# Two FFNs with 512-column up matmuls, a convolution that reads SBUF, one-tensor decay levels and other banks for the first output projection

## What is computed

```python
def first_block(x, ...):
    ...
    og = gla_attention(gq, gk, gv, split_heads(log_a, GLA_HEADS))      # gated linear attention
    ...
    x = x + jnp.concatenate([y_moba, y_gla], axis=-1) @ w_out[l]       # output projection, "out1"
    hn = rms_norm(x, ffn_norm_g[l])
    h = causal_dwconv(hn @ w_ffn_up[l], conv_w[l], conv_b[l])          # 1024 -> 2 * 2816, then 3 taps over tokens
    h_gate, h_val = h[..., :D_FF], h[..., D_FF:]
    x = x + (jax.nn.silu(h_gate) * h_val) @ w_ffn_down[l]              # "ffn1"
    return rms_norm(x, final_norm_g)

def _swiglu(x, w_in, w_out):                                           # second block, "ffn2"
    g, u = jnp.split(x @ w_in, 2, axis=-1)
    return (jax.nn.silu(g) * u) @ w_out
```

## Time and profile before

| | |
|---|---|
| time, median of 3 runs (lowest to highest) | 782.22 us (782.15 to 782.26) |
| the profiled execution: its time, its span | 782.25 us, 780.4 us |
| TensorE clock granted, mean over the span | 0.988 of full speed |
| busy: TensorE matmul, weight load, VectorE, ScalarE, GpSimd | 753.9, 707.7, 468.2, 371.2, 56.6 us |
| chain that ended last: TensorE, VectorE, ScalarE | 91%, 5%, 2% |

### The profile page before, as it was taken

How to read it: one execution, slowest core, us unless ns; L and a number is a source line. 1 busy time by engine, 2 the same in 40 slices (tenths; PEclk the granted TensorE clock), 3 DMA queues, 4 the chain that set the end, 5 groups by cost and what they waited for, 6 DMA issues and landing times.

```text
span 780.4 us, 13423 instructions
## 1 busy us (share of the span) xinstructions
PE 753.9 (97%) x5562; PEld 707.7 (91%) x5562; DVE 468.2 (60%) x533; ACT 371.2 (48%) x441; POOL 56.6 (7%) x63
## 2 busy tenths in 40 slices
PE   8999894999999999999999999999999999999997
PEld 8898883799999999989989999999989999999996
DVE  5669744457667677677447645565675544454542
ACT  6535354346454554555555563544435343434331
POOL 2465400010000000003000000000010000000000
PEclk9999996999999999999999999999999999999999
DMA  8733331335445455542442444445443554545431
GB/s 331 300 108 128 143 110 54 115 113 205 163 167 209 166 210 182 197 162 89 182 162 108 165 160 168 173 167 195 170 179 134 174 206 162 202 174 198 180 108 54
DMA packets 18046, 128.30 MB, mean 164 GB/s; under 512 B 2000, under 2 KB 2256, under 8 KB 2768
## 3 DMA queue, kind: packets, MB, share of 16 engines
q1 hardware_dynamic: 18000, 127.63, 45.3%
HBM read 126.57 MB, written 1.05 MB: 164 GB/s over the span
## 4 chain that ended last, share of the span: by engine, by line
PE 91%; DVE 5%; ACT 2%; issue 1%; POOL 1%; DMA 1%; SPq 0%; DVEq 0%; ACTq 0%
PE ps L1373 29%; PE ps L1374 28%; PE ps L1375 28%; PE ps L1362 1%; DVE low L900 1%; PE ps L1480 1%; DVE h L930 1%; PE ps L1517 1%; DMA cst<-in_cst 1%; PE ps L1510 0%; DVE xlo L947 0%; PE ps L1489 0%; ACT xhi L561 0%; PE ps L1656 0%; POOL st L476 0%
## 5 line engine op out<-in xcount | busy, mean ns | idle before, releaser
L900 DVE TENSOR_TENSOR low<-raw,hiw 128x2048 fp32r<-128x2048 f32 x116 | 271.1, 2338 | 200.1 <-ACT hiw L531 199.7
L1373 PE MATMUL ps<-xhi,hiw 128*128 128x256 f32 x1216 | 346.4, 285 | 3.5 <-DVE xlo L947 1.8
L1374 PE MATMUL ps<-xlo,hiw 128*128 128x256 f32 x1216 | 344.0, 283 | 0.0
L1375 PE MATMUL ps<-xhi,low 128*128 128x256 f32 x1216 | 344.0, 283 | 0.0
L531 ACT ACTIVATE hiw<-raw 128x2048 fp32r<-128x2048 f32 x116 | 221.4, 1911 | 89.8 <-PE ps L1375 89.8
L1373 PEld LDWEIGHTS ps<-xhi,hiw 128*128 128x128 f32 x1216 | 232.9, 192 | 6.5 <-DVE arena L1323 1.9
L1374 PEld LDWEIGHTS ps<-xlo,hiw 128*128 128x128 f32 x1216 | 233.0, 192 | 0.7
L1375 PEld LDWEIGHTS ps<-xhi,low 128*128 128x128 f32 x1216 | 233.0, 192 | 0.0
L1373 PE MATMUL ps<-hiw,yhi 128*128 128x512 f32 x208 | 82.7, 398 | 10.4 <-ACT arena L621 10.4
L1374 PE MATMUL ps<-low,yhi 128*128 128x512 f32 x208 | 82.2, 395 | 0.0
L1375 PE MATMUL ps<-hiw,ylo 128*128 128x512 f32 x208 | 81.9, 394 | 0.0
(11 more groups left out here) (193 smaller groups left out, 723.3 us busy)
## 6 DMA issues: line engine op xcount, KB each, us to landing
raw<-in_slabs SPq DMA_DIRECT2D x117, 1024.0 KB, 4.7
vec<-in_vec SPq DMA_DIRECT2D x1, 1258.5 KB, 9.6
cst<-in_cst SPq DMA_DIRECT2D x1, 1220.0 KB, 13.7
h<-in_x SPq DMA_DIRECT2D x2, 512.0 KB, 3.9
out<-h SPq DMA_DIRECT2D x2, 512.0 KB, 2.6
vec<-in_vec SPq DMA_DIRECT2D x1, 229.0 KB, 5.1
cst<-in_cst SPq DMA_DIRECT2D x1, 66.0 KB, 4.1
```

The costliest lines, as they stand in the source:

```text
L900: dve.tensor_tensor(low[:, n % SPLIT, :], raw[:, n % RAW, :], hiw[:, n % SPLIT, :].bitcast(F32), ALU.subtract).then_inc(lo_made, 1)
L1373: pe.matmul(o, whi, mhi, start=start, stop=False)
L1374: pe.matmul(o, whi, mlo, start=False, stop=False)
L1375: return pe.matmul(o, wlo, mhi, start=False, stop=stop)
```

## The change

- Output projection: the accumulators take banks 0, 1, 3, 4, and the four tiles of the norm behind it banks 2, 5, 6, 7.
- Levels: keys and queries are scaled in place in one tensor, the early half of each block by the keys and the late half by the queries, 256 columns each; `Kl` is gone and TensorE reads both operands from `Dl`.
- Both FFNs: `xhi` and `xlo` become two slices of one tensor `xx`, side by side. An up slab makes for each column half and contraction tile one matmul of 512 columns (high weights by both) and one of 256 columns (low weights by `xhi`, added to the first half of the bank). A hidden tile so takes two banks: 4 and 5 for gate, 6 and 7 for value, in every step. VectorE adds the two halves by a `tensor_reduce` of 1024 columns to 512 in SBUF and gives the banks back.
- First FFN: all three taps then read SBUF (`hid`). Second FFN: silu and product read SBUF (`up`).

```diff
+OUT1_BANKS = (0, 1, 3, 4)
...
-        xhi = sb("xhi", [P, KT, T], F32R)
-        xlo = sb("xlo", [P, KT, T], F32R)
+        xx = sb("xx", [P, KT, 2, T], F32R)
+        xhi, xlo = xx[:, :, 0, :], xx[:, :, 1, :]
...
-            tenant(f"w1_{q}", q, 0)
+            tenant(f"w1_{q}", OUT1_BANKS[q], 0)
         for q in range(4):
-            tenant(f"n1_{q}", 4 + q, 2)
+            tenant(f"n1_{q}", (2, 5, 6, 7)[q], 2)
...
-        FREE = {"ffn1": 2, "ffn2": 1}
+        FREE = {"ffn1": 1, "ffn2": 1}
...
-                    tenants[4 + 2 * (f % 2) + j].append(FREE[k])
+                    tenants[4 + 2 * j].append(FREE[k])
...
-        def hidden(k, f, j):
-            return ps[:, 4 + 2 * (f % 2) + j, :]
+        def wide_hidden(j):
+            return ps[:, 4 + 2 * j:6 + 2 * j, :]
...
                 pool.wait_ge(s("decay"), i + 1)
-                pool.tensor_tensor(Kl[i % 2], Dl[i % 2], gkT, ALU.mult)
-                pool.tensor_tensor(Dl[i % 2], Dl[i % 2], gqT, ALU.mult).then_inc(s("level_scaled"), 1)
+                early, late = level_halves(Dl[i % 2], i)
+                pool.tensor_tensor(early, early, level_halves(gkT, i)[0], ALU.mult)
+                pool.tensor_tensor(late, late, level_halves(gqT, i)[1], ALU.mult).then_inc(s("level_scaled"), 1)
...
-                    act.wait_ge(*hidden_full(k, f, j, i))
                     if k == "ffn1":
+                        act.wait_ge(*hidden_free(k, f, j, i))
...
-                            act.activation(yb[par][:, 2 * j + c, :], hidden(k, f, j)[:, c * T:(c + 1) * T],
+                            act.activation(yb[par][:, 2 * j + c, :], hid[par][j][:, c, :],
                                            ACT.Identity, scale=sc, bias=bi).then_inc(s("tap2"), 1)
                     elif j == 0:
-                        act.activation(sil[par], hidden(k, f, 0), ACT.Silu).then_inc(hidden_free(k, f, 0)[0], 1)
+                        act.wait_ge(*hidden_free(k, f, 0, i))
+                        act.activation(sil[par], up[par][0].rearrange("p a b -> p (a b)"), ACT.Silu)\
+                           .then_inc(s("silu_made2"), 1)
...
                     if k == "ffn1":
 
+                        dve.wait_ge(*hidden_full(k, f, j, i))
+                        dve.tensor_reduce(hid[par][j], wide_hidden(j).rearrange("p c (a b) -> p c b a", a=2), AX_X,
+                                          ALU.add).then_inc(hidden_free(k, f, j)[0], 1)
+                        dve.wait_ge(*hidden_free(k, f, j, i))
                         for c in range(2):
...
-                            dst, src = yb[par][:, 2 * j + c, :], hidden(k, f, j)[:, c * T:(c + 1) * T]
+                            dst, src = yb[par][:, 2 * j + c, :], hid[par][j][:, c, :]
...
+                    else:
+                        dve.wait_ge(*hidden_full(k, f, j, i))
+                        if f >= 2 and j == 0:
+                            dve.wait_ge(s("silu_made2"), f - 1 if i is None else f - 1 + 2 * i)
+                        dve.tensor_reduce(up[par][j], wide_hidden(j).rearrange("p c (a b) -> p c b a", a=2), AX_X, ALU.add)\
+                           .then_inc(hidden_free(k, f, j)[0], 1)
...
-                    dve.tensor_tensor(gt[par], hidden(k, f, 1), sil[par], ALU.mult).then_inc(hidden_free(k, f, 1)[0], 1)
+                    dve.wait_ge(s("silu_made2"), f + 1 if i is None else f + 1 + 2 * i)
+                    dve.wait_ge(*hidden_free(k, f, 1, i))
+                    dve.tensor_tensor(gt[par], up[par][1].rearrange("p a b -> p (a b)"), sil[par],
+                                      ALU.mult).then_inc(s("gated2"), 1)
...
+            def feature_major_wide(banks, n, norm=None):
+
+                hi, lo = slab_views(n, KT)
+                for c in range(2):
+                    o = banks[:, c, :]
+                    cc_ = slice(c * P, (c + 1) * P)
+                    for kt in range(KT):
+                        turned(norm if c == 0 else None, kt)
+                        both = xx[:, kt].rearrange("p a b -> p (a b)")
+                        if kt < KT - 1:
+                            pe.matmul(o, hi[:, kt, cc_], both, start=kt == 0, stop=False)
+                            pe.matmul(o[:, 0:T], lo[:, kt, cc_], xhi[:, kt, :], start=False, stop=False)
+                        else:
+                            pe.matmul(o[:, 0:T], lo[:, kt, cc_], xhi[:, kt, :], start=False, stop=False)
+                            mm = pe.matmul(o, hi[:, kt, cc_], both, start=False, stop=True)
+                return mm
...
-                    q_, k_ = Dl[i % 2], Kl[i % 2]
+                    q_ = k_ = Dl[i % 2]
...
-                    if i is not None or f >= 2 or ffn_lease[k][2 * (f % 2) + j][1]:
-                        pe.wait_ge(*hidden_free(k, f, j, i, done=False))
+                    pe.wait_ge(*hidden_free(k, f, j, i, done=False))
...
-                    feature_major(hidden(k, f, j), n + j, norm if (f, j) == (0, 0) else None).then_inc(hidden_full(k, f, j)[0], 1)
+                    first = norm if (f, j) == (0, 0) else None
+                    up_made = feature_major_wide(wide_hidden(j), n + j, first)
+                    up_made.then_inc(hidden_full(k, f, j)[0], 1)
```

More of the change, by code:

```diff
@@ L352, in build @@
         Dl = [piece(512 * j, 2, T) for j in range(2)]
-        Kl = [piece(1024 + 512 * j, 2, T) for j in range(2)]
         zb, za, ze = (piece(3072 + 512 * j, 2, T) for j in range(3))
@@ L373, in build @@
         gt = [piece(7168 + 512 * j, 512) for j in range(2)]
+        hid = [[piece(8192 + 1024 * j + 512 * k, 2, T) for j in range(2)] for k in range(2)]
+        up = [[piece(4096 + 1024 * j + 512 * k, 2, T) for j in range(2)] for k in range(2)]
         sg = piece(0, 2, KT, T)
```

44 lines of the change are left out of this document (24 added, 20 removed).

## The result

The changed kernel takes 798.12 us (median of 4 runs, 797.30 to 801.42), the kernel before 782.18 (4 runs on the same chip, 782.10 to 782.26): ratio 1.0212, 95% interval 1.0182 to 1.0242. It is 2.1% slower. The forecast was 788.3 with a range up to 797.0: the sign came out, the size did not. The profiled execution took 798.81, its span is 797.0, 16.6 us more than before.

The account below looks back on a forecast made before the run. TensorE's own pace bounds the FFNs before; after the change a VectorE-ScalarE chain bounds the first FFN. From 782.25 us, -12.5 - 3.8 - 4.2 + 24.5 + 2.0 = +6.0 gives 788.3 us, range 781 to 797.

Parts of the forecast that it names:

- Banks, -12.5: Output projection: first slab no longer waits for bank 2, the second starts 12.5 us sooner, clock stays at 2.4 GHz; -12.5 us.
- What follows has the same waits as before: Output projection behind the second slab: a further transpose, two slabs and the norm keep their waits, so 12.5 us is saved.
- Levels, -3.8: Last attention levels: shorter GpSimd products let VectorE deliver sooner, -2.3 us of wait, and the clock doesn't fall; -3.8 us.
- The clock's share: Last levels: TensorE's clock, which fell to half behind the wait, was expected not to fall, worth 1.5 us.
- a wait under 0.6 us: Sign named for the levels: TensorE's wait in the last levels, 2.41 us before, falls under 0.6 us.
- 512-column matmuls in the second FFN, -4.2: Second FFN up slabs: 0.205 us less a slab, 4.5 us in 22 slabs, less 0.3 for tight banks; -4.2 us.
- The price of the tight spots (0.3): Second FFN: up(1) after reduce(0) and up(10) value after reduce(9) wait for single banks; 0.3 us for both.
- First FFN, +24.5 and +2.0: First FFN: VectorE-ScalarE chain of 19.0 us a loop step against TensorE's 16.6, +24.5 us; lower clock at last down slab, +2.0.
- two taps 0.93 (0.505 each): First FFN chain: ScalarE's pair of convolution taps takes 0.93 us, 0.505 each with a little overlap.
- the walk: First FFN chain followed step by step, 18.1 us straight and 19.0 in the loop, until down(10) ends at 374.4 instead of 349.9.
- The rivals with a cheap sum: First FFN: reduce under 0.95 us instead of 1.22; at 0.69 the time is 776.6, or 772.5 with register stops hidden; chance 0.14.
- Half of the projection's gain lost: Output projection rival: its second wait, or the clock, keeps half of the 12.5 us, giving 794.5; counted within slower, 0.78.

## Why the prediction was off

**Banks, -12.5: measured -11.4.** In the changed kernel the first slab started at 115.66, 11.5 us sooner than in the earlier trace rows, the second at 123.02, 13.65 sooner (both include the levels' gain and the later start-up). "What follows has the same waits as before" was wrong. With the slabs early, slab 15's low part on VectorE stood ahead of the third pair of heads, and the values behind them waited 1.1 us more. Moving the heads ahead brought 1.14 us.

**Levels, -3.8: measured -3.1.** The clock's share was right (1.5). The wait shrank by 1.32 in place of 2.3: the prediction let GpSimd be done before VectorE's remainder started, and it still overlapped two instructions of VectorE. The sign named on record, a wait under 0.6 us, did not come.

**512-column matmuls in the second FFN, -4.2: measured -2.5.** A mixed tile takes 0.353 us where 0.347 was taken: 16 x 0.006 is 0.1 of the 0.205 us a slab. The spacing behind a wide up matmul is 237 ns, not the 227 of the down slabs. It is 237 also where another wide one follows, so it isn't the mix of widths that costs the 10 ns; what does isn't shown. The price of the tight spots (0.3) can't be told apart from it. The formula of the Trainium skill, page "TensorE: Matmul & The Clock Gate", section "Back-to-back issue gap", weighed in the prediction, gave 0.9 for this FFN; the measured 2.5 lies about half-way between it and the forecast.

**First FFN, +24.5 and +2.0: measured +31.6.** The mechanism was right in its main steps: a sum of 1.22 us (1217 and 1220 ns measured), a chain across VectorE and ScalarE that nothing can pass, TensorE waiting for `low` twice a step, 5.1 us without a start ahead of the last down slab (5.6 worked out), and the clock low behind it. Against the record, TensorE also waited twice for a pair of banks (4.5 us, near the end), but for the same late VectorE. The last down slab took 7.5 us (361.54 to 369.04) where its pace is 5.45, 2.05 more. That this hits the +2.0 is partly luck: the same slab was 1.7 to 2.9 us over its pace in the other kernels here that waited ahead of it for over 4 us. The step of the prediction that failed here is the term "two taps 0.93 (0.505 each)". The price was taken from a line without a bias; the taps have one and take 595 ns, the pair 1.10. With the bias left out the loop step is 18.94 and the straight one 18.2, against 19.0 and 18.1 on record, and the last down slab starts 206.3 us after the first up slab, against 205.9 on record (368.9 - 162.97). That is 4.7 of the 5.1 us that were missed here; the other 0.4 is within what the walk can tell (its straight step is put at 18.1, while the items listed for it add up to 17.9). The row was in sight: the same taps from PSUM, two operands, took 554 ns in the kernel before, and were not set against L591, a read of PSUM with one operand and 472 ns.

**The start-up, 0 against +1.75.** In the profiled execution of the kernel after, TensorE's clock was half over the start-up's first matmuls. Of the ten experiments' profiled executions four show this too (13.5 to 13.8) and six 11.8 to 12.3. All five slow ones are of kernels with `xx`, none of the three kernels without it is; but four kernels with `xx` started fast, so the edit alone does not bring it. Besides, the kernel before falls into two groups of times: on two chips 9 of its 22 runs beside the experiments took 781.8 to 782.6 us and 13 took 783.4 to 784.0, some 1.6 apart; on a third chip 9 runs spread over 782.1 to 784.9. That fits a start-up that varies from one execution to the next, but those runs have no trace, and the cause stays open. Without the 1.75 the profiled execution would have stood at 797.1, at the edge of the range on record.

**The sum.** Measured stage by stage: -14.2 - 2.5 + 31.6 = +14.9, and +1.75 for the start-up. On record: -20.5 + 26.5 = +6.0. Of the 8.9 us between them 5.1 are the first FFN, 4.7 of it what leaving the bias out took back, and 3.8 the gains taken too high (1.7 in the second FFN, 2.1 in the attention). The rivals with a cheap sum fell by the reduce's 1217 ns. "Half of the projection's gain lost" was nearest to the truth there, with 1.1 of 12.5. The range's upper end was made from a dearer sum alone; no price was left open for the taps, though their place (22 pairs on the chain) gave each 0.1 us the weight of 2.2.

## What to carry to other kernels

When a sum or copy is put between a producer and two engines that work on it in turn, look first at the order in their queues: here the same work with two low parts moved into the gaps made 228 us into 201. Price an instruction from a row with the same kinds of operands, and give every item that stands n times on a chain a range of its own, since its error comes back n times. When a long wait goes, walk the queues behind it too: what was early enough before comes behind something else now.
